# Differential attention with 64-row score contractions, one maximum and one ratio per head, and rotary and output gate moved ahead of the value products

## Chip, core and metric

The kernel runs on one core of a Trainium2 chip. All arithmetic is float32 in the matmuls. The metric is the device time of one execution in microseconds, lower is better; before the change the median of 3 runs is 1255.58 us (1250.82 to 1259.35).

## What is computed

A transformer block over 256 latent tokens and 256 context tokens of width 1024 (a token mixer of differential attention beside a gated recurrence, then 16 experts), followed by a second block (MLA and Fourier branches) that the change does not touch. Of the first mixer this matters here:

```python
def diff_attend(q, k, v, lam):       # 4 heads x 2 branches, head dim 64, value dim 128
    s = jnp.einsum("bhiqd,bhikd->bhiqk", q, k).astype(jnp.float32) * (DA_HEAD_DIM ** -0.5)
    p = jax.nn.softmax(s, axis=-1)
    a = p[:, :, 0] - lam * p[:, :, 1]
    return jnp.einsum("bhqk,bhkd->bhqd", a.astype(v.dtype), v)

q = apply_axial_rope(qk_heads(da_q), cos, sin)            # x*cos + rotated(x)*sin
k_all = concatenate([k_ctx, apply_axial_rope(qk_heads(da_k), cos, sin)])     # 512 keys
out_da = merge_heads(rmsnorm(o_da, da_subln) * (1.0 - lambda_init))
out_hg = merge_heads(rmsnorm(o_hg_lat, hg_norm)) * jax.nn.silu(hg_g)
y_lat = jnp.concatenate([out_da, out_hg], axis=-1) @ w_out
```

## The kernel before

Every engine has its own program, written out in order by hand; engines meet through semaphores. Eight PSUM banks of 128x512 float32 are handed out ahead of time: `claim(name, bank)` gives each use of a bank a turn, `pe_take` makes TensorE wait until the previous user of the bank has been copied (`freed`), `wait_filled` makes a reader wait for TensorE (`filled`), `wait_copied` waits for the copy. `pclaim` goes round banks 0 to 3.

Weights come as 2 MB tiles (128 x 8 x 512 float32) through SyncE's queue, which works through `stream` in order: tile i goes to ring slot i % 4 and is issued once the last reader of tile i-4 has run. Slots 4 and 5 are scratch (`scr`: gates, decays, `XFB`, `gb`) until the experts.

The mixer runs on TensorE in this order. After the gates, the recurrence's levels (`level(0)` to `level(7)`) are interleaved with the key and query projections and with `mod_step(k)`, which are products of the modulation matrix (`w_ada`, columns). Then come the value projection (`("v", b)`, weight tile 2), `cross` and `oh` (the recurrence's output), `mod_step(12)`, the rotation products `rot` (a constant 128x128 matrix against q and k), the output gate's projection `g` (weight tile 7), and the attention loop over `da`: 2 blocks of 128 queries x 4 heads, n = 0 to 7.

In the loop the step of head n is, on TensorE: four transposes of the weights a (`aT`), the scores of head n+2, `mod_gate(n-1)` (a row product of the modulation), the value product `o`, a piece of context work for the second block (`c2T`, `kvc`, `kvcT`, `kpcT`), and `mod_product(n)` (L778, a 2 MB tile of `w_ada`). ScalarE: copies `aT`, takes the two exponentials of head n+2 (L1440, with row sums), at a block's last head the four squares of `o`, context copies, and the copy of the modulation product (`take_mod`). VectorE: `da_difference(n+1)` (L1923 to L1929), `da_max(n+2)` (L1881, L1883), at n = 0 `output_gate(1)`, then `gate_rows(n-1)` (L1892, L1895), which frees the bank of `mod_gate`, and at a block's last head the norm of `o` (L1951), which waits for GpSimd's inverse root.

Each score of a branch contracts all 128 partitions: q lies with both branches one above the other, and `qh` and `smat` hold copies in which the other branch's 64 rows are zero. Two maxima and two reciprocals are taken for a head. The output gate is made from an exponential (L1426), a sum with 1, a reciprocal over 128x512 (L1584) and two multiplications per token block.

After the loop the mixed rows are transposed (`mixT`) and multiplied by `w_out` (`y`), the router runs, and from about 473 us 16 experts follow in a loop whose first iteration's weights are already in the ring and whose later ones stream in at about 410 GB/s.

## Time and profile before

| | |
|---|---|
| runs | 1255.58 us median, 1250.82 to 1259.35 |
| profiled execution, its own time | 1254.22 us |
| its span in the trace | 1252.4 us |
| TensorE busy over the span | 977.6 us (78%) |
| TensorE busy, 245 to 312 us (values, recurrence out, rotary, gate) | 61.11 of 67.00 us |
| TensorE busy, 312 to 394 us (attention loop) | 67.06 of 82.00 us |
| experts, 473 to 1180 us | DMA at 305 GB/s on average, 410 in most slices |
| VectorE, ScalarE, GpSimd busy over the span | 420.1, 208.9, 48.2 us |

"PEclk" in the windows is TensorE's granted clock as a share of full speed (1.0 is 2.4 GHz, 0.5 is 1.2 GHz). In a timeline a row is a merged run of like instructions: its start, its length, engine, line, operation, output<-input, shapes, count, and in brackets how long the engine had stood idle before it and who released it.

### The profile page before, as it was taken

To read this page: it belongs to the slowest core of one execution; us is meant where nothing else is said; L and a number is where in the kernel's file an instruction comes from. 1 tells how busy PE (TensorE), PEld (TensorE's weight loads), DVE (VectorE), ACT (ScalarE), POOL (GpSimd) and SP (SyncE) were. 2 spreads that over 40 slices of the span, in tenths; PEclk is the share of its full clock that TensorE was granted. 3 is DMA by queue.
4 is the path that set the end of the run, shared out by engine and by line. 5 is a ranking of instruction groups with operands and counts; after the bars stand their busy time and mean duration, and the time that the engine had idled before them with its cause. 6 is when DMAs were issued, how large, how long until landed. Compare 5 with 4: busy or idle time off the path is not lost.

```text
span 1252.4 us, 11145 instructions
## 1 busy us (share of the span) xinstructions
PE 977.6 (78%) x4368; PEld 483.6 (39%) x4368; DVE 420.1 (34%) x643; ACT 208.9 (17%) x426; POOL 48.2 (4%) x101
## 2 busy tenths in 40 slices
PE   4799989998887777566666666666665998998987
PEld 2666456654443442111111111111112764544843
DVE  1398244616741342111111111111224264411422
ACT  2123132312441211000000000000002033301010
POOL 0100000001010100000000000000001000000000
PEclk9899989998898878877777777777777999998999
DMA  9934253844639507999999999999997441023000
GB/s 355 330 134 167 102 201 133 304 153 150 231 133 391 211 1 283 410 409 410 410 409 410 410 410 410 409 410 410 409 410 289 155 152 68 1 85 117 1 1 33
DMA packets 102230, 310.44 MB, mean 248 GB/s; under 512 B 2705, under 2 KB 4932, under 8 KB 102068
## 3 DMA queue, kind: packets, MB, share of 16 engines
q1 hardware_dynamic: 99700, 301.04, 62.4%
q0 software_dynamic: 2496, 8.93, 2.0%
q8 instruction: 23, 0.38, 0.1%
q14 instruction: 11, 0.09, 0.0%
HBM read 308.91 MB, written 1.05 MB: 247 GB/s over the span
## 4 chain that ended last, share of the span: by engine, by line
PE 57%; DMA 29%; DVE 7%; SPq 2%; issue 2%; ACT 1%; POOL 1%; POOLq 0%; ACTq 0%; DVEq 0%
PE bank L760 39%; DMA ring<-w_up_dram 27%; PE bank L1091 7%; PE bank L778 3%; DMA ring<-w_ada_dram 2%; SPq L659 1%; PE bank L768 1%; PE bank L889 1%; PE bank L1107 1%; PE bank L788 1%; PE bank L974 1%; SPq L644 1%; PE bank L1196 1%; DVE state L2045 1%; PE bank L1219 1%
## 5 line engine op out<-in xcount | busy, mean ns | idle before, releaser
L1091 PE MATMUL bank<-ring,ilat 128*32 128x512 f32 x1024 | 140.4, 699 | 48.2 <-DMA ring<-w_up_dram 48.2
L1107 PE MATMUL bank<-ring,ilat 128*32 128x512 f32 x512 | 95.7, 915 | 11.7 <-ACT ilat L1507 11.7
L760 PE MATMUL bank<-ring,hT 128*128 128x512 f32 x224 | 101.9, 616 | 3.7 <-DVE gates L1850 2.0
L760 PE MATMUL bank<-ring,kT 128*128 128x512 f32 (+1 forms) x224 | 97.8, 598 | 5.2 <-DVE kT L1616 3.4
L2043 DVE TENSOR_SCALAR state<-state 64x512 f32<-64x512 f32 x16 | 6.7, 419 | 256.9 <-ACT state L1505 256.9
L1091 PEld LDWEIGHTS bank<-ring,ilat 128*32 128x32 f32 x1024 | 35.3, 124 | 149.0 <-issue 92.1
L1098 PE MATMUL bank<-const,state 128*128 128x128 f32 x64 | 17.9, 434 | 95.7 <-DVE state L2049 95.7
L760 PE MATMUL bank<-hT,ring 128*128 128x256 f32 (+1 forms) x320 | 86.4, 431 | 3.6 <-DVE hT L1654 3.6
L760 PEld LDWEIGHTS bank<-hT,ring 128*128 128x128 f32 x320 | 61.6, 194 | 28.3 <-issue 17.7
L1119 PE MATMUL bank<-state,ilat 128*128 128x512 f32 x128 | 58.7, 602 | 14.6 <-DVE state L2051 14.6
L760 PEld LDWEIGHTS bank<-ring,hT 128*128 128x128 f32 x224 | 43.9, 198 | 59.2 <-issue 57.3
L760 PEld LDWEIGHTS bank<-ring,kT 128*128 128x128 f32 x224 | 43.2, 194 | 58.3 <-issue 58.3
L778 PE MATMUL bank<-ring,act 128*32 128x512 f32 x384 | 51.5, 661 | 8.3 <-DMA ring<-w_ada_dram 5.6
L760 PE MATMUL bank<-kT,ring 128*128 128x256 f32 x256 | 55.7, 379 | 0.0
L1098 PEld LDWEIGHTS bank<-const,state 128*128 128x128 f32 x64 | 11.5, 217 | 112.0 <-DVE state L2049 112.0
L2051 DVE COPY state<-bank 128x512 f32<-128x512 f32 x16 | 11.1, 692 | 127.4 <-PE bank L1107 127.4
L2045 DVE RECIPROCAL state<-state 64x512 f32<-64x512 f32 x16 | 53.5, 3345 | 0.5
L1505 ACT ACTIVATE state<-bank 64x512 f32<-64x512 f32 x16 | 9.4, 590 | 262.3 <-PE bank L1091 262.3
L1107 PEld LDWEIGHTS bank<-ring,ilat 128*32 128x32 f32 x512 | 21.3, 158 | 78.0 <-issue 77.1
L760 PEld LDWEIGHTS bank<-kT,ring 128*128 128x128 f32 x256 | 48.6, 190 | 7.3 <-issue 0.8
L1119 PEld LDWEIGHTS bank<-state,ilat 128*128 128x128 f32 x128 | 23.0, 189 | 51.6 <-issue 51.6
L768 PE MATMUL bank<-const,pair 128*128 128x128 f32 x112 | 21.8, 361 | 26.6 <-DVE pair L1982 19.0
(319 smaller groups left out, 1096.3 us busy)
## 6 DMA issues: line engine op xcount, KB each, us to landing
ring<-w_down_dram SPq DMA_DIRECT2D x32, 2048.0 KB, 19.9
ring<-w_gate_dram SPq DMA_DIRECT2D x32, 2048.0 KB, 18.9
ring<-w_up_dram SPq DMA_DIRECT2D x32, 2048.0 KB, 23.0
ring<-w_ada_dram SPq DMA_DIRECT2D x24, 2048.0 KB, 11.6
ring<-w_in_dram SPq DMA_DIRECT2D x8, 2048.0 KB, 13.3
ring<-fno_w_in_dram SPq DMA_DIRECT2D x4, 2048.0 KB, 8.8
ring<-w_out_dram SPq DMA_DIRECT2D x2, 2048.0 KB, 15.5
ring<-mla_w_in_dram SPq DMA_DIRECT2D x2, 2048.0 KB, 21.8
```

What stands on the lines that cost most here:

```text
L644: sp.dma_start(slot_view(s, src.shape[1], src.shape[2]), src).then_inc(landed[s], 16)
L659: sp.dma_start(expert_view(s), expert_src(w, e, half)).then_inc(landed[s], 16)
L760: ins = pe.matmul(o, l, r, start=start and i == 0, stop=stop and i == len(terms) - 1)
L768: ins = pe.transpose(o[:, jj * P:(jj + 1) * P], src[:, j * P:(j + 1) * P], ident)
L778: ins = pe.matmul(o[32 * q:32 * q + 32, :], act_cols[i // 12][:, j, :], w[:, j, :], start=jj == 0, stop=jj == 1)
L788: ins = pe.matmul(o[:, 2 * jj:2 * jj + 2], x[:, jj * P:(jj + 1) * P], C("sum_columns"), start=True, stop=True)
L889: ins = pe.matmul(o[:, k * P:(k + 1) * P], keys[:, c:c + P], queries[:, c:c + P], start=True, stop=True)
L1091: ins = pe.matmul(bank[0][32 * t:32 * t + 32, :], xin_cur[:, j, :], w[2 * half + t // 2][:, j % JH, n0:n0 + TN], start=j == 0, stop=j == J ...
L1098: ins = pe.transpose(bank[1][:, k * P:(k + 1) * P], hidden_rows[:, k * P:(k + 1) * P], ident)
L1107: ins = pe.matmul(bank[2 + n][32 * q:32 * q + 32, :], hmT[:, q, 32 * c:32 * c + 32], w[4 + c][:, q, n * TN:(n + 1) * TN], start=c == 0, st ...
L1119: ins = pe.matmul(bank[4 + 2 * b + n][:, :], s_cur[:, b * P:(b + 1) * P], yb[n], start=False, stop=last)
L2045: dve.reciprocal(eg, eg).then_inc(hidden, 1)
```

## The change

Scores: each branch contracts its own 64 partitions of q and k directly (`q3[ps]`, `k3[ps]`, rows 0 to 63 and 64 to 127). The zero-padded copies and the memsets that made them are gone. The two score banks of a head are adjacent, so that one reduction over 2 x 512 gives both maxima and one exponent pair waits for it. The difference is scaled by one ratio: a' = p0 - lam*(s0/s1)*p1, not divided by s0; the RMS norm removes the factor s0, with EPS scaled by s0*s0 (`eps_sums`) in GpSimd's root.

Order: `rot` and `g` move ahead of the value projection, with weight tiles 7 and 2 swapped in the stream, and `mod_step(12)` and the first two heads' scores ahead of `cross` and `oh`. The rotary arithmetic moves ahead of `cross_ready` on VectorE. The gate becomes tanh: (1+tanh(x/2))*x*0.5*hg_norm, and is applied in the multiplication that normalises `oh` (`recurrent_out`), which moves into VectorE's loop iteration n = 0. `kvctx` leaves the four-slot ring for slot 4, so the `w_ada` tiles of heads 4 to 7 are loaded one head earlier. `o` moves to banks 5 and 6, context work to 6 and 5, the modulation products of the loop to bank 7. The squares and norm of `ctx_2`, and its load, move to the values stage and earlier.

```diff
-        for i, (name, _) in enumerate(stream):
-            place(name, i % EARLY_SLOTS)
+        for name, _ in stream:
+            if name[0] == "kvctx":
+                place(name, EARLY_SLOTS)
+            else:
+                place(name, turn % EARLY_SLOTS)
+                turn += 1
...
         for b in range(TB):
-            if b:
-                claim(("o", b), 7)
+            claim(("o", b), 5 + b)
             for h in range(HEADS):
                 n = b * HEADS + h
                 claim(("aT", b, h), 4)
-                if n == 0:
-                    claim(("o", 0), 6)
                 for name in context_work[n]:
-                    claim(name, 4 if name == ("kpcT",) else 5)
-                claim(("mod", GATE_MODS[n]), 7 - b)
-                claim(("gt", GATE_MODS[n]), 7 - b)
+                    claim(name, 4 if name == ("kpcT",) else 6 - b)
+                claim(("mod", GATE_MODS[n]), 7)
+                claim(("gt", GATE_MODS[n]), 7)
...
# TensorE
             def da_scores(b, h):
+                o = [pe_take(pe, ("s", b, h, i)) for i in range(2)]
                 for i in range(2):
-                    o = pe_take(pe, ("s", b, h, i))
-                    fills(pe.matmul(o[:, :], qz[i][:, h * T + b * P:h * T + (b + 1) * P], k3[:, h, :],
-                                    start=True, stop=True), ("s", b, h, i))
+                    ps = slice(64 * i, 64 * i + 64)
+                    fills(pe.matmul(o[i][:, :], q3[ps, h, b * P:(b + 1) * P], k3[ps, h, :],
+                                    start=True, stop=True), ("s", b, h, i))
...
# ScalarE
+            da_exp(0)
+            act.wait_ge(sem("rstd_c2"), 1)
+            act.wait_ge(sem("c2_normed"), TB)
+            for b in range(TB):
+                o = wait_filled(act, ("oh", b))
+                for h in range(HEADS):
+                    square(o[:, h * P:(h + 1) * P], 4 * b + h, P, (b, h) == (TB - 1, HEADS - 1))
...
-            da_exp(0)
             da_exp(1)
...
# VectorE
             def da_max(n):
                 for i in range(2):
-                    o = wait_filled(dve, ("s",) + da[n] + (i,))
-                    c = (2 * n + i) % 4
-                    step(dve.tensor_reduce(mx[:, 4 + c:5 + c], o[:, :], AX, ALU.max))
-                    st.settle()
-                    step(dve.tensor_scalar(mx[:, c:c + 1], mx[:, 4 + c:5 + c], -DH ** -0.5, None, ALU.mult), "da_max")
+                    wait_filled(dve, ("s",) + da[n] + (i,))
+                c = 2 * (n % 2)
+                step(dve.tensor_reduce(mx[:, 4 + c:6 + c],
+                                       score_banks[n % 2][:, :].rearrange("p (i t) -> p i t", i=2), AX, ALU.max))
...
-                step(dve.reciprocal(cf[:, c:c + 2], rs[:, c:c + 2]))
+                c = 2 * (n % 2)
+                step(dve.reciprocal(cf[:, c:c + 1], da_sums[:, 8 + n:9 + n]))
                 st.settle()
-                step(dve.tensor_tensor(cf[:, 4 + c:5 + c], cf[:, c + 1:c + 2], lamc, ALU.mult))
+                step(dve.scalar_tensor_tensor(cf[:, c + 1:c + 2], cf[:, c:c + 1], da_sums[:, n:n + 1], lamc,
+                                              ALU.mult, ALU.mult))
                 st.settle()
-                step(dve.tensor_scalar(pbuf[c + 1], pbuf[c + 1], cf[:, 4 + c:5 + c], None, ALU.mult))
-                st.settle()
-                step(dve.scalar_tensor_tensor(pbuf[c], pbuf[c], cf[:, c:c + 1], pbuf[c + 1], ALU.mult, ALU.add),
+                step(dve.scalar_tensor_tensor(pbuf[c], pbuf[c + 1], cf[:, c + 1:c + 2], pbuf[c], ALU.mult, ALU.add),
                      "a_ready")
...
                 if n == 0:
-                    output_gate(1)
+                    recurrent_out()
```

In TensorE's program of the kernel before, from the end of `mod_step(12)` to the first transposes (L788 is the modulation's column product, L962 `rot`, L760 here `g`, L974 the scores):

```order
L788 MATMUL bank<-const,modr 128x2 x4
L962 MATMUL bank<-qT,const 128x256 x4
L962 MATMUL bank<-kT,const 128x256 x4
L760 MATMUL bank<-ring,hT 128x512 x16
L974 MATMUL bank<-kT,qh 128x512
L974 MATMUL bank<-kT,smat 128x512
```

In TensorE's program of the changed kernel, from the last level (L907) to `cross` (L973); L942 is `rot`, the first L778 row `g` and the first two blocks of values, L959 the four scores of heads 0 and 1:

```order
L907 MATMUL bank<-qh,ring 128x128 x8
L942 MATMUL bank<-qT,const 128x256 x4
L942 MATMUL bank<-kT,const 128x256 x4
L778 MATMUL bank<-ring,hT 128x512 x32
L806 MATMUL bank<-const,vda 128x2 x4
L796 MATMUL bank<-ring,act 32x512 x8
L778 MATMUL bank<-ring,hT 128x512 x16
L806 MATMUL bank<-const,modr 128x2 x4
L959 MATMUL bank<-kT,qT 128x512 x4
L973 MATMUL bank<-ring 128x128 x8
```

What stood between the recurrence's output and the loop now stands before it: `cross` and `oh` follow the first scores directly, and the first transposes follow `oh`.

In ScalarE's program of the changed kernel, from the copies of `cross` (L1434) to the copy of the first modulation product of the loop (L1334); L1446 are the exponentials, L1299 the squares of `oh`, L1471 the copy of `aT`:

```order
L1434 ACTIVATE ring<-bank 128x512 x2
L1446 ACTIVATE gates,small<-bank,small 128x512 x2
L1299 ACTIVATE junk,small<-bank 128x128 x8
L1446 ACTIVATE gates,small<-bank,small 128x512 x2
L1471 ACTIVATE gates<-bank 128x512
L1446 ACTIVATE gates,small<-bank,small 128x512 x2
L1334 ACTIVATE gates<-bank 128x512
```

The squares of `oh` now stand between the exponentials of head 0 and those of head 1; before, they stood ahead of both and four copies of the gate's projection lay between.

In VectorE's program of the changed kernel, from the maximum of head 2 (L1895) to the difference of head 2 (L1935 to L1940); L1881 is the eightfold normalisation and gating of `oh`:

```order
L1895 TENSOR_REDUCE small<-bank 128x2
L1898 TENSOR_SCALAR small<-small 128x2
L1881 SCALAR_TENSOR_TENSOR pair<-bank,small,ring 128x128 x8
L1887 MEMSET small 128x1
L1935 RECIPROCAL small<-small 128x1
L1937 SCALAR_TENSOR_TENSOR small<-small 128x1
L1940 SCALAR_TENSOR_TENSOR gates<-gates,small 128x512
```

Where the gate's sum, reciprocal and multiplications stood (L1582 to L1872 of before), the reading of `oh` out of banks 6 and 7 stands now.

## Rows read from the trace of the kernel before

**Rows 1.** Windows: length; PE, PEld, DVE, ACT, POOL busy; PEclk, DMA share, GB/s.

```profile
245.00:312.00 67.00, 61.11 (x230) 33.96 (x230) 26.95 (x38) 12.57 (x32) 5.60 (x7) 0.95 0.49 173
312.00:394.00 82.00, 67.06 (x341) 34.94 (x340) 42.74 (x99) 33.88 (x90) 8.00 (x14) 0.88 0.64 223
473.00:1180.00 707.00, 513.07 (x2437) 214.75 (x2436) 177.86 (x238) 77.16 (x164) 20.72 (x47) 0.84 0.77 305
```

**Rows 2.** Timeline of TensorE before the loop: start, length, line, shapes, idle before.

```profile
245.49 13.90 PE L760 MATMUL bank<-ring,hT 128*128 128x512 f32 x32
292.49 1.10 PE L962 MATMUL bank<-kT,const 128*128 128x256 f32 x4 [3.15 <-DVE modc L1637]
295.60 16.82 PE L760 MATMUL bank<-ring,hT 128*128 128x512 f32 x32 [2.01 <-DVE gates L1850]
```

**Rows 3.** Timeline of TensorE in the loop.

```profile
318.41 1.11 PE L1004 MATMUL bank<-const,gates 128*128 128x128 f32 x4 [2.56 <-DVE gates L1929]
332.45 3.39 PE L778 MATMUL bank<-ring,act 128*32 128x512 f32 x16 [2.77 <-DVE hT L1892]
335.78 0.66 PE L1004 MATMUL bank<-const,gates 128*128 128x128 f32 x4
342.12 0.66 PE L1004 MATMUL bank<-const,gates 128*128 128x128 f32 x4
342.62 1.02 PE L974 MATMUL bank<-kT,qh 128*128 128x512 f32 x2
346.62 1.92 PE L778 MATMUL bank<-ring,act 128*32 128x512 f32 x16
348.47 0.66 PE L1004 MATMUL bank<-const,gates 128*128 128x128 f32 x4
354.64 1.13 PE L760 MATMUL bank<-vda,gates 128*128 128x128 f32 x8 [2.93 <-DVE hT L1892]
```

**Rows 4.** The same, from the last head to the output product.

```profile
376.15 0.66 PE L1004 MATMUL bank<-const,gates 128*128 128x128 f32 x4
382.49 2.94 PE L778 MATMUL bank<-ring,act 128*32 128x512 f32 x16 [2.27 <-DMA ring<-w_ada_dram]
389.94 3.65 PE L768 MATMUL bank<-const,pair 128*128 128x128 f32 x16 [1.60 <-DVE qT L1912]
394.58 1.95 PE L760 MATMUL bank<-ring,kT 128*128 128x512 f32 x4 [0.99 <-ACT kT L1474]
```

**Rows 5.** Windows with and without a lowered clock.

```profile
295.00:302.00 7.00, 6.40 (x9) 2.75 (x10) 6.90 (x8) 2.30 (x4) 1.83 (x2) 0.55 0.03 8
336.00:354.00 18.00, 15.71 (x86) 7.84 (x84) 11.89 (x30) 11.53 (x33) 1.27 (x2) 1.00 0.90 312
```

**Rows 6.** Timeline of ScalarE and VectorE, end of the levels.

```profile
246.90 1.22 DVE L1815 TENSOR_TENSOR ring<-gates 128x1024 f32<-128x1024 f32 x1
249.64 0.58 ACT L1317 ACTIVATE vda<-bank 128x512 f32<-128x512 f32 x1
```

**Rows 7.** Timeline of ScalarE, VectorE and GpSimd: pieces of a head's chain.

```profile
344.54 0.69 DVE L1881 TENSOR_REDUCE small<-bank 128x1 f32<-128x512 f32 x1
340.38 0.16 DVE L1923 RECIPROCAL small<-small 128x2 f32<-128x2 f32 x1
341.30 0.75 DVE L1929 SCALAR_TENSOR_TENSOR gates<-gates,small 128x512 f32<-128x512 f32 x1
344.65 0.69 ACT L1440 ACTIVATE gates<-bank,small 128x512 f32<-128x512 f32 x1 [1.24 <-DVE small L1883]
290.12 2.16 DVE L1837 SCALAR_TENSOR_TENSOR pair<-bank,small,hgn 128x128 f32<-128x128 f32 x8 [29.75 <-POOL small L695]
348.33 1.04 POOL L695 TENSOR_TENSOR small<-small 128x4 f32<-128x4 f32 x1
```

**Rows 8.** DMA issues of GpSimd: KB each, us to landing.

```profile
state<-norm_post_ffn_dram POOLq DMA_DIRECT2D x1, 512.0 KB, 6.8
```

**Rows 9.** Chain that ended last, at the loop's end.

```profile
374.39 8.05 DMA ring<-w_ada_dram
```

More of the change, by code:

```diff
@@ L174, in block_program @@
         ident = C("ident")
-        bank = [ctx.enter_context(nc.psum_tensor(f"bank{b}", [P, TN], F32)) for b in range(8)]
+        score_banks = [ctx.enter_context(nc.psum_tensor(f"bank{2 * i}", [P, 2 * TN], F32)) for i in range(2)]
+        bank = [x[:, i * TN:(i + 1) * TN] for x in score_banks for i in range(2)]
+        bank += [ctx.enter_context(nc.psum_tensor(f"bank{b}", [P, TN], F32)) for b in range(4, 8)]
         filled = [sem(f"filled{b}") for b in range(8)]
@@ L337, in block_program @@
         ecol = small[:, 96:128]
+        da_sums = small[:, 96:112]
+        eps_sums = small[:, 112:116]
         lbt = small[:, 128:152]
@@ L418, in block_program @@
         claim_levels(7)
+        for s in range(2):
+            for n in range(2):
+                pclaim(("rot", s, n))
+        for b in range(TB):
+            pclaim(("g", b))
         pclaim(("v", 0))
@@ L429, in block_program @@
             lb_turn[0] += 1
-        claim_mod(12)
-        for s in range(2):
-            for n in range(2):
-                pclaim(("rot", s, n))
-        for b in range(TB):
-            pclaim(("g", b))
         context_work = [(), (("c2T", 0, 0),), (("c2T", 0, 1),), (("c2T", 1, 0),), (("c2T", 1, 1),),
@@ L712, in _ @@
             root_inverse(TB, TB, "rstd_in")
+            for b in range(TB):
+                wait_filled(pool, ("dsum", 1, b))
+            pool.dma_start(c2, a["ctx_2"][0].rearrange("(b p) d -> p b d", p=P)).then_inc(sem("ctx2_in"), 16)
+            root_inverse(0, TB, "rstd_c2")
+            wait_filled(pool, ("v", 2 * TB - 1))
+            for i, row in enumerate((a["b_ada"][0, 2 * D:3 * D], a["b_ada"][0, 5 * D:6 * D],
+                                     a["b_ada_2"][0, 2 * D:3 * D], a["b_ada_2"][1, 2 * D:3 * D])):
+                pool.dma_start(G[i], row.partition_broadcast(P)).then_inc(sem("post_in"), 16)
             wait_filled(pool, ("oh", TB - 1))
@@ L914, in _ @@
             level(7)
+            for s, x in enumerate((q3, k3)):
+                for n in range(2):
+                    if s == 0:
+                        wait_copied(pe, ("q", n))
+                    else:
+                        wait_copied(pe, ("k", 2 * n))
+                        wait_copied(pe, ("k", 2 * n + 1))
+                    o = pe_take(pe, ("rot", s, n))
+                    for i in range(2):
+                        ins = pe.matmul(o[:, i * T:(i + 1) * T], C("rotate"), x[:, 2 * n + i, 0:T],
+                                        start=True, stop=True)
+                    fills(ins, ("rot", s, n))
+            w = wait_tile(pe, ("in", 7))
+            for b in range(TB):
+                tokens_out(("g", b), w, hT3, b)
             w = wait_tile(pe, ("in", 2))
@@ L1403, in _ @@
             take_mod(COLUMN_MODS[10])
+            for b in range(TB):
+                o = wait_filled(act, ("g", b))
+                st.did(act.activation(gb[:, b * TN:(b + 1) * TN], o[:, :], ACT.Tanh, scale=0.5), sem("gb_tanh"))
             for b in range(2 * TB):
@@ L1408, in _ @@
                     take_mod(COLUMN_MODS[11])
+                    act.wait_ge(sem("ctx2_in"), 16)
+                    for i in range(TB):
+                        square(c2[:, i, :], i, D, i == TB - 1)
             for d in range(2):
@@ L1464, in _ @@
                     if b == 0:
-                        act.wait_ge(sem("rstd_c2"), 1)
+                        act.wait_ge(sem("rstd_oh"), 1)
+                        for i in range(TB):
+                            wait_copied(act, ("oh", i))
                     for i in range(HEADS):
@@ L1830, in _ @@
                                        .broadcast_to([P, HEADS, P]), ALU.mult), "state1_ready" if d else None)
+            for b in range(TB):
+                g_ = gb[:, b * TN:(b + 1) * TN]
+                dve.wait_ge(sem("gb_tanh"), b + 1)
+                frees(st, dve.scalar_tensor_tensor(g_, g_, 1.0, bank[turns[("g", b)][0]][:, :], ALU.add, ALU.mult),
+                      ("g", b))
+                st.settle()
+                g4 = g_.rearrange("p (h n) -> p h n", h=HEADS)
+                step(dve.scalar_tensor_tensor(g4, g4, 0.5, hgn[:, :].rearrange("p (h n) -> p h n", h=1)
+                                              .broadcast_to([P, HEADS, P]), ALU.mult, ALU.mult))
@@ L1912, in take_context @@
                     frees(st, dve.tensor_copy(kp_ctx, o[:, 0:T]), ("kpcT",))
-            dve.wait_ge(sem("rstd_c2"), 1)
-            for b in range(TB):
-                step(dve.tensor_scalar(c2[:, b, :], c2[:, b, :], rr[:, b:b + 1], None, ALU.mult), "c2_normed")
             def da_difference(n):
```

172 lines of the change are left out of this document (73 added, 99 removed).

## Prediction

> **What bounds the kernel now.** I read the windows by stage first. In the two stages that the change touches TensorE is busy 61.11 of 67 us and 67.06 of 82 us, with the granted clock at 0.95 and 0.88 of full speed, while VectorE has 26.95 and 42.74 us of work [rows 1]. So TensorE's program sets the pace, and what can be won is its idle time, the time at a lowered clock, and work taken from it. The experts behind are another matter: 707 us in which DMA moves 305 GB/s [rows 1] and whose weights are asked for as the previous ones are used up. Their start follows the end of the mixer one for one, so a microsecond won before 394 us is one won at the end.
>
> Next the timeline of TensorE. Ahead of the loop it idles 3.15 us because the last `rot` product needs a bank that VectorE has not emptied, and 2.01 us in front of `g` for the same reason; `g` then takes 16.82 us where the first half of the value product, the same 32 instructions, takes 13.90 [rows 2]. The window shows why: the clock is at 0.55 of full speed there, between the levels 1.2 and 2.4 GHz, and at 1.00 where no such gap stands [rows 5]. At the loop's start it idles 2.56 us for the first difference, in head 1 2.77 us (`output_gate(1)` with its long reciprocal holds up `gate_rows`), in head 4 2.93 us [rows 3]. After two of these gaps the modulation product takes 3.39 instead of 1.92 us, or the start of a head is stretched likewise [rows 3]. Heads 2 and 3 have no wait: 335.78 to 342.12 to 348.47, so 6.35 us is what one head's work costs [rows 3]. At the end the last modulation product waits 2.27 us for its tile, asked for only at 374.39 and 8.05 us under way [rows 4, 9], then runs slow (2.94), and `mixT` needs 3.65 us for 16 transposes after a wait of 1.60 [rows 4].
>
> **The change, step by step.** I carry TensorE's position from 245.49 us and compare it at four marks.
>
> *Up to the first transposes (before: 318.41).* The work on TensorE is the same as before except the scores. Before, idle time is 3.15 + 2.01 + 2.56 [rows 2, 3], and the slow `g` cost 16.82 - 13.90 = 2.9. Gone is 10.6 us. New waits: the fourth `rot` product needs the bank of modulation product 10, which ScalarE copies at 249.64 + 0.58 = 250.2, behind the exponentials that wait for VectorE at 246.90 + 1.22 [rows 6]. Three `rot` products of 0.86 us from 245.5 end at 248.1, so 2.2 us idle. A gap of 2.2 us lies near the 2.0 and 2.8 that went with a lowered clock [rows 2, 3]; I count 1.5 us for that. The scores of two heads: one of 512 columns lasts 0.86 us (its two passes are 1.02 with the tail [rows 3]). The two branches now use separate halves of the array's rows. The nearest row is the modulation product: 16 instructions of 512 columns on separate groups of 32 columns last 1.92 us in all [rows 3], 0.12 each, where one on the full array costs 0.43; four run side by side. So I take it that the halves overlap: 0.86 instead of 1.72 us per head, here -1.7. Both ends for each head: 0 and -0.86. The rotary arithmetic on VectorE (six operations, 7.4 us) and the gate's (four of 0.75) lie under 41 us of `g` and value products; without that cover they would cost 10 us. Sum: -10.6 + 2.2 + 1.5 - 1.7 = -8.6, and half a microsecond for the slow start of head 0 (its transposes took 1.11 instead of 0.66 [rows 3]); the maximum, exponential and difference of head 0 now lie under `oh`. Mark: 309.3, **-9.1**.
>
> *Heads 0 and 1 (before: 318.41 to 335.78, 17.4).* The bulk of VectorE's gate arithmetic is gone, with the waits of 2.77 and the slow clock after it. In its place: `oh` is complete at 309.3 and everything of the loop hangs on ScalarE. Squares of the second `oh` 1.6, exponentials of head 1 1.6 (two of 0.69 with accumulator reads [rows 7]), copy of `aT` 0.6: 313.1, so the value product of head 0 waits 2.4 us. VectorE has the exponentials at 312.5, the difference 1.15 (0.16 + 0.16 + 0.75 and gaps [rows 7]), the maximum of head 2 over 2x512 elements: 1.4 (the row of 512 takes 0.69, of which some 0.15 is fixed; between 1.2 and 1.4 [rows 7]), then the eight multiplications of `oh`, 2.16 by the row of the same form [rows 7], to 317.4. These free bank 7, for which modulation product 0 waits: before, `oh` was out of bank 7 at 292. So TensorE idles a further 2.5 us there, and 1.5 us goes for the clock. GpSimd's root (1.04 for four columns [rows 7], up to 2 for eight) stands behind three DMA issues, ends at about 313.5 and is not the last. Modulation product 0 ends at 320.9, head 1 takes 5.5 us: 326.5. That is 17.2 us, **-0.2**: one stall was traded for another.
>
> *Heads 2 to 6 (before: 335.78 to 376.15, 40.4).* Heads 2 and 3 lose 0.8 each by the overlapped scores; head 5 too. Head 4 keeps its stall. The chain is squares of `o`, root (1.04 [rows 7] and the sum ahead of it, 1.4), four multiplications and then difference, maximum and `gate_rows(3)`. It starts 0.6 us later on ScalarE against TensorE than before because both exponentials now wait for both scores, but what waits for it is no longer `o` but the modulation product, 1.3 us further on, and VectorE's pieces are 0.7 us shorter. I get an idle of 1.35 + 1.71 instead of 2.93, without a single long gap: -2.6, the slow clock included. Head 6: 0. Mark: 362.0, together **-4.9**.
>
> *End of loop to output product (before: 376.15 to 394.58, 18.4).* The tile of the last product is now asked for after head 3 instead of head 4, so 25 us ahead: -2.27 and the slow product -1.1. The row product behind it no longer lies at the lower clock (-1.2). The wait for the last copies (1.60) and for ScalarE (0.87, 0.99) stay. `mixT` at full speed would take 1.9 instead of 3.65; since these small gaps stay I count half. **-6.3**.
>
> Sum: -9.1 - 0.2 - 4.9 - 6.3 = -20.5. From the execution's own 1254.2 us: 1233.7. The median of the runs lies 1.4 above the profiled one: **1235 us**.
>
> Priced at nothing, with their cover: the tanh (ScalarE's program as built holds no table load more than before, and ScalarE is busy 12.57 of 67 us in this stage [rows 1]), the load of `ctx_2`, now at about 128 us, and its squares and norm, under the value product; at the loop's start they would cost 5 us.
>
> **The rivals.**
>
> *The two score products do not overlap.* For it: no row here has a contraction of 64, only column groups. The Trainium skill, "TensorEngine Tiling (Array Packing)", Key Properties, states that tiles execute in parallel, but also that changing the tiling mode drains the engine. By the first rule the sum stands at -20.5; by the second each head, which now changes mode twice more, would pay for it. The trace bears the drain out little: head 2's 6.35 us hold two changes to 128x32 and back and add up from the single rows without a remainder above 0.1 us [rows 3]. Without overlap all scores together cost 0.86 x 8 = 6.9 more; some of it falls into waits that exist anyway (2 us), leaving 5: 1240 us.
>
> *Fewer stalls than counted.* The gaps of 2.2 and 2.5 us leave the clock alone and `mixT` runs fast: 1.5 + 1.5 + 0.9 us more: 1231 us.
>
> *The new order's waits cost more at head 0 and in each block.* ScalarE carries in each head a copy, two exponentials that start only after a reduction over both banks, a context copy of 1.5 and the modulation copy: 4.9 of 5.5 us. If these slip by 1.2 us in six heads and with them the clock: +9 us, 1244 to 1248, within 1%.
>
> *Slower than before.* `gate_rows(0)` waits for six broadcast loads, two of which GpSimd issues only after `oh`, now 309.5 us, with the router's and the 768 KB context tile behind them. The slower of them was seen to land after 6.8 us [rows 8], so at 317, and is wanted at 324. Every microsecond past 324 holds bank 7, and with it TensorE, one for one. It decides when the landing takes 20 us more than wanted (344, no gain left), and makes 1268 us when it lands at 357. A whole 2 MB tile took 8.05 us [rows 9]; three such ahead of the rows would put the landing at 334, which costs 10 us and does not yet reach the old time.
>
> **How the numbers follow.** My sum 0.50; no overlap 0.18; fewer stalls 0.14; more waits 0.14; slower 0.04. Within 1% of 1255.6 is 1243 to 1268, about what a measurement of this kernel can tell from no change. Faster: the first three, 0.82 less 0.02 for their tails; same: the fourth and these tails, 0.16; slower 0.04. The range takes the fast rival's 1231 less 3 for the spread of runs, and up to the middle of the fourth: 1228 to 1245.
>
> **What the profile will show.** Right: the first transposes at 308 to 311 us, the output product's start at 372 to 377, score pairs of 0.9 to 1.1 us for both branches, the last modulation product without a DMA wait. At head 0 a wait of 2 us or more for ScalarE's copy and another on the VectorE row that normalises `oh`. Wrong: pairs of 1.7 us; a wait in `cross` for the rotary arithmetic; a wait of `gate_rows(0)` for DMA; an expert loop that does not move with the mixer's end.

## The result, and the profile after

The changed kernel takes 1235.58 us (median; 1234.59 to 1237.53), against 1254.62 us (1250.82 to 1259.35) for the kernel before beside it: a ratio of 0.985, 95% interval 0.981 to 0.989, so 19 us or 1.5% faster. Forecast were 1235 us and 1228 to 1245. The profiled execution has a span of 1232.8 us (before 1252.4) and its own time of 1234.59. How much of the agreement is merit is the subject of what follows: in the part of the program that the change touches the sum had promised 20.5 us and 16.8 came.

The windows of the changed kernel (length; busy time of PE, PEld, DVE, ACT, POOL; PEclk, DMA share, GB/s), to be held against [rows 1]:

```profile
245.00:312.00 67.00, 64.06 (x250) 35.83 (x249) 23.73 (x34) 13.81 (x36) 4.38 (x9) 0.97 0.51 185
312.00:379.00 67.00, 54.47 (x326) 29.86 (x327) 30.79 (x75) 30.20 (x85) 7.21 (x12) 0.92 0.91 329
473.00:1180.00 707.00, 509.43 (x2438) 224.64 (x2430) 184.15 (x242) 79.27 (x167) 19.95 (x45) 0.86 0.76 299
```

From 312 us to the output product are now 67 us instead of 82 (the second window ends where that stage ends), with 12.5 us of TensorE idle instead of 15, at 0.92 of full clock instead of 0.88; VectorE's work in this window fell from 42.74 to 30.79 us. These windows don't hold the same work: at 312 us the kernel before had only reached the first scores, the changed one was past the first transposes. So the 15 us are not the gain of the loop; the table below compares like with like. The experts' window has hardly changed.

TensorE's timeline of the changed kernel (start, length, line, shapes, count, idle before and its releaser), which answers to [rows 2] to [rows 4]:

```profile
250.81 2.05 PE L942 MATMUL bank<-kT,const 128*128 128x256 f32 x4 [2.12 <-ACT vda L1334]
...
298.33 1.99 PE L959 MATMUL bank<-kT,qT 64*128 64x512 f32 x8
300.25 2.05 PE L973 MATMUL bank<-ring 128*128 128x128 f32 x16
...
310.25 0.60 PE L1021 MATMUL bank<-const,gates 128*128 128x128 f32 x4
310.78 1.13 PE L959 MATMUL bank<-kT,qT 64*128 64x512 f32 x4
314.10 1.16 PE L778 MATMUL bank<-vda,gates 128*128 128x128 f32 x8 [2.19 <-ACT gates L1471]
318.42 3.64 PE L796 MATMUL bank<-ring,act 128*32 128x512 f32 x16 [3.16 <-DVE pair L1881]
...
328.07 0.66 PE L1021 MATMUL bank<-const,gates 128*128 128x128 f32 x4
328.66 1.13 PE L959 MATMUL bank<-kT,qT 64*128 64x512 f32 x4
329.72 1.13 PE L814 MATMUL bank<-modr,const 128*128 128x512 f32 x2
330.68 1.05 PE L778 MATMUL bank<-vda,gates 128*128 128x128 f32 x8
...
342.41 1.10 PE L814 MATMUL bank<-modr,const 128*128 128x512 f32 x2 [0.85 <-ACT modr L1334]
346.25 1.92 PE L796 MATMUL bank<-ring,act 128*32 128x512 f32 x16 [1.42 <-DVE hT L1907]
...
364.17 0.66 PE L1021 MATMUL bank<-const,gates 128*128 128x128 f32 x4
368.17 1.92 PE L796 MATMUL bank<-ring,act 128*32 128x512 f32 x16
373.68 3.58 PE L786 MATMUL bank<-const,pair 128*128 128x128 f32 x16 [1.60 <-DVE qT L1927]
378.25 3.24 PE L778 MATMUL bank<-ring,kT 128*128 128x512 f32 x7 [0.99 <-ACT kT L1488]
```

In place of the 3.15 and 2.01 us ahead of the loop stands one gap of 2.12, in place of 2.56 and 2.77 in heads 0 and 1 stand 2.19 and 3.16, in place of 2.93 in head 4 stand 0.85 and 1.42, and the wait of 2.27 for a tile at the end is gone.

The start of a kernel differs from one trace to the next (the last level, from which I count below, starts between 243.6 and 249.0 us in twelve traces), and so do the experts. Only the changed kernel was traced twice, with starts 0.26 us apart, so whether the start goes by the execution or by the kernel is not shown. Places in the mixer are compared by their distance from the start of the last level, 243.60 us before and 244.05 after; these distances are called marks below.

| mark: us from the last level to | before | after | stage before | stage after | stage forecast |
|---|---|---|---|---|---|
| transposes of head 0 | 74.81 | 66.20 | | -8.6 | -9.1 |
| transposes of head 2 | 92.18 | 84.02 | 17.37 | 17.82 (+0.45) | -0.2 |
| transposes of head 7 | 132.55 | 120.12 | 40.37 | 36.10 (-4.3) | -4.9 |
| output product `y` | 150.98 | 134.20 | 18.43 | 14.08 (-4.35) | -6.3 |

The mixer gained 16.8 us. From `y` to the first expert it is 79.09 and 79.04 us, so the experts' start followed one for one. The other 3 us of this trace come from the experts, 2.3 of them from TensorE's clock in the last one (its down product took 6.19 and 5.60 us, and the up product as follows); the same products of that expert before (L1091) and after (L1108), from the two timelines:

```profile
931.78 5.34 PE L1091 MATMUL bank<-ring,ilat 128*32 128x512 f32 x32 [3.37 <-DMA ring<-w_up_dram]
```

```profile
914.81 3.64 PE L1108 MATMUL bank<-ring,ilat 128*32 128x512 f32 x32 [2.70 <-DMA ring<-w_up_dram]
```

The shapes and the count are the same and the change doesn't touch the line; after a wait for the tile of 3.37 us it ran slow in one trace, after one of 2.70 at full clock in the other (in the earlier experts of the changed kernel's trace the up products run slow and fast by turns). From the first expert to the last one's final product it is 478.12 us before and 475.24 after; in the ten other traces 475.1 to 477.8, in no order with the mixer's length.

### The profile page after: what moved, and what is told of

The parts are those of the page before. It is cut to its first block, busy times and chain, and to the rows that moved or that the text cites. A ratio compares the mean times of both kernels' runs of the same rounds, so it can differ in the third digit from the quotient of the medians.

```text
span 1232.8 us, 11161 instructions
## 1 busy us (share of the span) xinstructions
PE 954.5 (77%) x4368; PEld 479.7 (39%) x4368; DVE 404.6 (33%) x615; ACT 206.4 (17%) x424; POOL 47.0 (4%) x101
## 3 DMA queue, kind: packets, MB, share of 16 engines
HBM read 308.91 MB, written 1.05 MB: 251 GB/s over the span
## 4 chain that ended last, share of the span: by engine, by line
PE 57%; DMA 29%; DVE 6%; SPq 3%; issue 2%; ACT 2%; POOL 1%; POOLq 0%; ACTq 0%; DVEq 0%
PE bank L778 39%; DMA ring<-w_up_dram 27%; PE bank L1108 7%; PE bank L796 3%; SPq L671 2%; DMA ring<-w_ada_dram 2%; PE bank L907 1%; PE bank L786 1%; PE bank L1124 1%; PE bank L806 1%; SPq L653 1%; PE bank L1213 1%; DVE state L2060 1%; PE bank L1236 1%; PE bank L1136 1%
## 5 line engine op out<-in xcount | busy, mean ns | idle before, releaser
L1108 PE MATMUL bank<-ring,ilat 128*32 128x512 f32 x1024 | 133.2, 668 | 57.7 <-DMA ring<-w_up_dram 57.7
L778 PE MATMUL bank<-ring,kT 128*128 128x512 f32 (+1 forms) x224 | 97.6, 597 | 5.4 <-DVE kT L1630 3.4
L778 PE MATMUL bank<-ring,hT 128*128 128x512 f32 x224 | 99.6, 605 | 1.7 <-DVE hT L1630 1.7
L1124 PE MATMUL bank<-ring,ilat 128*32 128x512 f32 x512 | 90.5, 872 | 11.8 <-ACT ilat L1521 11.8
L1108 PEld LDWEIGHTS bank<-ring,ilat 128*32 128x32 f32 x1024 | 35.5, 121 | 153.0 <-issue 153.0
L778 PE MATMUL bank<-hT,ring 128*128 128x256 f32 (+1 forms) x320 | 86.6, 432 | 3.6 <-DVE hT L1668 3.6
L778 PEld LDWEIGHTS bank<-hT,ring 128*128 128x128 f32 x320 | 62.0, 196 | 28.3 <-issue 17.7
L778 PEld LDWEIGHTS bank<-ring,kT 128*128 128x128 f32 x224 | 43.1, 194 | 58.0 <-issue 58.0
L778 PEld LDWEIGHTS bank<-ring,hT 128*128 128x128 f32 x224 | 43.5, 195 | 56.1 <-issue 54.0
L778 PE MATMUL bank<-kT,ring 128*128 128x256 f32 x256 | 55.7, 379 | 0.0
L1115 PEld LDWEIGHTS bank<-const,state 128*128 128x128 f32 x64 | 11.4, 217 | 110.1 <-DVE state L2064 110.1
L778 PEld LDWEIGHTS bank<-kT,ring 128*128 128x128 f32 x256 | 48.7, 190 | 7.2 <-issue 0.8
L1124 PEld LDWEIGHTS bank<-ring,ilat 128*32 128x32 f32 x512 | 20.5, 154 | 73.6 <-issue 72.7
## 6 DMA issues: line engine op xcount, KB each, us to landing
ring<-w_down_dram SPq DMA_DIRECT2D x32, 2048.0 KB, 20.5
```

Source lines behind the costliest of these rows:

```text
L778: ins = pe.matmul(o, l, r, start=start and i == 0, stop=stop and i == len(terms) - 1)
L1108: ins = pe.matmul(bank[0][32 * t:32 * t + 32, :], xin_cur[:, j, :], w[2 * half + t // 2][:, j % JH, n0:n0 + TN], start=j == 0, stop=j == J ...
L1115: ins = pe.transpose(bank[1][:, k * P:(k + 1) * P], hidden_rows[:, k * P:(k + 1) * P], ident)
L1124: ins = pe.matmul(bank[2 + n][32 * q:32 * q + 32, :], hmT[:, q, 32 * c:32 * c + 32], w[4 + c][:, q, n * TN:(n + 1) * TN], start=c == 0, st ...
```

## The experiments

My theory: each stall is set by one instruction of another engine that stands behind work nobody waits for, and the change traded six of them (3.15 + 2.01 + 2.56 + 2.77 + 2.93 + 2.27 = 15.7 us) for five (2.12 + 2.19 + 3.16 + 0.85 + 1.42 = 9.7 us), beside the overlapped scores. First rival: the gain is nearly all work taken from TensorE, and the waits float, that is, a wait that is removed comes back at the next place, so that moving one instruction moves nothing. Second rival: what counts is the clock, and waits matter only where they lower it. Kernels with "from before" are the kernel before with one part of the change; the others are the changed kernel with one edit.

### Scores over 128 rows again

```diff
-                    fills(pe.matmul(o[i][:, :], q3[ps, h, b * P:(b + 1) * P], k3[ps, h, :],
+                    fills(pe.matmul(o[i][:, :], q3[:, h, b * P:(b + 1) * P], k3[:, h, :],
```

> The changed kernel with both score products of a head contracting all 128 rows (both branches get the same scores, so the output differs); instruction shapes are those of the kernel before, all else as changed. Theory: the two 64-row halves run side by side, so a head's pair now lasts 0.96 to 1.06 us and would last 1.72 again: +1.5 us for heads 0 and 1 ahead of the recurrence's output, nothing for head 2 (TensorE waits there anyway), +0.66 for most of heads 3 to 7. The output product starts 4 to 5 us later (382 to 383 us) and the time is 1239 to 1241 us. Rival, the loop's pace is set by ScalarE and VectorE: under 2 us later, 1236 to 1238 us.

1241.72 us (1239.87 to 1242.12), a ratio to before of 0.989 (0.987 to 0.992): 4 to 6 us behind the changed kernel's two medians (1235.58 above, 1237.57 below). This kernel serves for its timing alone: it leaves out the separation of the two branches. TensorE in head 2, and `mixT` at the end:

```profile
332.50 0.66 PE L1021 MATMUL bank<-const,gates 128*128 128x128 f32 x4
333.00 1.88 PE L959 MATMUL bank<-kT,qT 128*128 128x512 f32 x4
334.72 1.02 PE L814 MATMUL bank<-modr,const 128*128 128x512 f32 x2
335.58 1.05 PE L778 MATMUL bank<-vda,gates 128*128 128x128 f32 x8
...
379.82 1.94 PE L786 MATMUL bank<-const,pair 128*128 128x128 f32 x16 [1.60 <-DVE qT L1927]
```

Start to start, both branches take 1.72 us here and 1.06 in the changed kernel (328.66 to 329.72); two heads in one go take 1.92 there (298.33 to 300.25). One head more costs 0.86, what one branch over 128 rows costs: the halves run fully side by side, and 0.20 us is paid once for each group. There is more around it: the scores start 0.59 us after the transposes instead of 0.50, and the row product behind them takes 0.96 instead of 0.86 (329.72 to 330.68, here 334.72 to 335.58). So going to 64 rows and back costs 0.20 + 0.09 + 0.10 = 0.39 us, and a head saves 0.46 us instead of 0.86. The Trainium skill, "TensorEngine Tiling (Array Packing)", Key Properties, says both that tiles run in parallel and that a change of mode drains the engine; this trace agrees with both: complete overlap, and 0.39 us for each excursion. That these 0.39 us are the drain is a reading; the trace shows only the time.

By the marks `y` is at 134.55, only 0.35 later than in the changed kernel. Heads 2 and 3 cost 1.24 us more (0.92 by the rows above, and 0.15 each ahead of the modulation product, which the kernel before did not have; I can't say why), heads 4 to 6 0.47, heads 0 and 1 0.36; against that the fourth `rot` product ran at full speed behind the same gap of 2.12 us (1.10 instead of 2.05), and `mixT` took 1.94 instead of 3.58 behind the same 1.60. With the clock set aside the 64 rows are worth about 3.4 us in this order, an estimate from these differences. The 4 to 5 us expected at `y` did not come in this trace; its 0.35 lies in the rival's range, but the rows show longer work on TensorE hidden by a higher clock, and not a pace set by other engines. This execution took 6.9 us longer than the changed kernel's profiled one, nearly all of it elsewhere: 4.3 us in the start-up, 0.5 in the experts and 2.2 in the second block, none of which the edit touches. So the trace does not explain the distance between the medians.

### The context tile back in the ring

```diff
-                if name[0] == "kvctx":
-                    wait_filled(sp, ("oh", TB - 1))
-                elif turn_of[name]:
+                if turn_of[name]:
```

(and the same condition taken out where the slots are placed.)

> The changed kernel with kvctx back in the ring of four slots. Theory: the tile of the last modulation product is again asked for only when kvctx's last reader has run (head 6), lands 8 us later, about 370.4, where it is wanted at 368.2: a DMA wait of 2.2 us in front of the last modulation product, a slow product behind it (2.9 us), output product 3 to 6 us later. Rival, the tile's wait is hidden by the copies at the loop's end: under 1 us.

One execution: 1242.93 us. All marks up to head 7 agree with the changed kernel within 0.03 us; then comes the wait:

```profile
372.17 3.50 PE L792 MATMUL bank<-ring,act 128*32 128x512 f32 x16 [2.17 <-DMA ring<-w_ada_dram]
```

`y` is at 137.84, 3.64 later: 2.17 of wait, 1.6 of slow product. The rest of the distance in time is start-up (1.7), experts (0.9) and the second block (2.2), which this edit doesn't reach.

### The copy of modulation product 10 first

```diff
+            take_mod(COLUMN_MODS[10])
             act.wait_ge(sem("end_distance"), 1)
...
-            take_mod(COLUMN_MODS[10])
```

> The changed kernel with ScalarE's copy of modulation product 10 ahead of its wait for the end distances. Theory: the wait of 2.12 us of the fourth rotation product goes, and with it the lowered clock behind it (1.7 us): first transposes 3.8 us earlier, about 306.4, time about 1232. Rival, the clock falls for another reason than the gap: 2.1 us earlier, with the rotation and gate products as slow as now.

One execution: 1235.46 us. The `rot` products now run without a gap:

```profile
249.69 1.03 PE L942 MATMUL bank<-kT,const 128*128 128x256 f32 x4
```

Head 0 is reached at 62.19 instead of 66.20: 4.0 us, 2.1 of wait and the rest the clock behind it; 3.9 of them still stand at `y`. The time doesn't show it, since this execution started 1.2 us later and its experts and second block took 1.2 and 2.2 us longer. By the marks it contradicts the first rival; the time alone, at 1235.46 us for about 1232 expected, would not.

### The gap at head 0 filled with unread products

```diff
                     context_product(*name)
+                if n == 0:
+                    for i in range(2):
+                        wait_copied(pe, ("s",) + da[1] + (i,))
+                    for i in range(3):
+                        pe.matmul(bank[2][:, :], q3[:, 0, 0:P], k3[:, 0, :], start=True, stop=True)
                 mod_product(GATE_MODS[n])
```

> The changed kernel with three matmuls of 512 columns that nothing reads put into the wait in front of modulation product 0. Theory: the idle gap of 3.16 us is what brings the clock down to 1.2 GHz; filled, the product takes 1.92 instead of 3.64 us and the next transposes 0.6 instead of 0.86: head 1 begins 1.9 to 2.0 us earlier. Rival, the clock comes down anyway: the product still takes over 3 us, nothing gained.

One execution: 1235.71 us.

```profile
318.38 2.74 PE L1039 MATMUL bank<-kT,qT 128*128 128x512 f32 x6
321.71 1.93 PE L796 MATMUL bank<-ring,act 128*32 128x512 f32 x16 [0.58 <-DVE pair L1886]
323.56 0.66 PE L1021 MATMUL bank<-const,gates 128*128 128x128 f32 x4
```

VectorE releases the bank no sooner (the modulation product starts 4.32 us after the value product, as without the edit), but it takes 1.93 instead of 3.64 us: heads 0 and 1 together 15.91 instead of 17.82, as expected. This separates the price of a wait from the price of the clock: the stall cost 3.16 us and 1.9 in clock.

### Head 0: exponentials first, root before the loads, norm of `oh` before the maximum

```diff
# ScalarE
             da_exp(0)
+            da_exp(1)
...
# GpSimd: ahead of the last three DMA issues
+            root_inverse(0, TB * HEADS, "rstd_oh")
             wait_filled(pool, ("oh", TB - 1))
...
# VectorE
-                if n + 2 < len(da):
-                    da_max(n + 2)
                 if n == 0:
                     recurrent_out()
+                if n + 2 < len(da):
+                    da_max(n + 2)
```

> The changed kernel with three pieces of order changed around head 0: ScalarE takes the exponentials of head 1 ahead of the squares of the recurrence's output, VectorE normalises that output ahead of the maximum of head 2, GpSimd takes its root ahead of three DMA issues. Theory: TensorE's two waits (2.19 and 3.16 us) are queue order on ScalarE, VectorE and GpSimd; bank 7 comes free about 2 us earlier and modulation product 0 starts at 316.4 instead of 318.4, still slow. Rival, squares and root are one chain that order doesn't shorten: under 1 us.

One execution: 1237.11 us.

```profile
315.37 1.16 PE L778 MATMUL bank<-vda,gates 128*128 128x128 f32 x8 [0.85 <-ACT gates L1471]
319.20 3.64 PE L796 MATMUL bank<-ring,act 128*32 128x512 f32 x16 [2.67 <-DVE pair L1881]
322.77 1.12 PE L1021 MATMUL bank<-const,gates 128*128 128x128 f32 x4
323.82 1.72 PE L959 MATMUL bank<-kT,qT 64*128 64x512 f32 x4
```

The value product waits 0.85 instead of 2.19, and with bank 7 free sooner the modulation product starts 6.34 us after head 0 instead of 8.17: the 2 us expected there, nearly. But the gap in front of the modulation product is still 2.67, since TensorE also arrives earlier, and the low clock now lasts into head 1 (1.12 and 1.72 for what took 0.86 and 1.13). Of 1.8 us won in the waits 0.97 is left at head 2. The three edits were made together, so what each gave is not shown.

### The last copies before the last gate row

```diff
-            gate_rows(len(da) - 1)
-
             take_context("kvcT")
             take_context("kpcT")
+
+            gate_rows(len(da) - 1)
```

> The changed kernel with VectorE's copies of kvcT and kpcT ahead of the last gate row. Theory: the transposes of the mixed rows wait 1.60 us for bank 4, which these copies free; they start 1.6 us earlier, and the output product 1.6 to 3.3 us earlier, depending on whether the clock stays up. Rival, another bank or ScalarE's copy decides: nothing.

One execution: 1234.94 us.

```profile
375.58 1.94 PE L786 MATMUL bank<-const,pair 128*128 128x128 f32 x16 [0.25 <-DVE qT L1927]
378.67 1.52 PE L778 MATMUL bank<-ring,kT 128*128 128x512 f32 x3 [1.15 <-ACT kT L1488]
```

Head 7 to `y` takes 11.26 instead of 14.08 us: 1.35 of the wait and 1.64 of `mixT` at full clock, less 0.16 of a longer wait for ScalarE. By the marks `y` comes 4.0 us earlier, but 1.66 of that lie ahead of head 0, where this trace has the same gap and a fast `rot` product (1.10 us); the edit has no part in it. This end was the same in both kernels; neither the change nor my forecast had touched VectorE's order there.

### From before: the context tile outside the ring, alone

```diff
+            if name[0] == "kvctx":
+                place(name, EARLY_SLOTS)
+            else:
+                place(name, turn % EARLY_SLOTS)
+                turn += 1
```

> The kernel before with only the ring changed: kvctx in slot 4, tiles of heads 4 to 7 one place earlier. Theory: the DMA wait of 2.27 us in front of the last modulation product goes, with its slow product (1.1) and part of what is slow behind it (1.2 and 1.8): 3.4 to 6 us, 1249 to 1251. Rival, hidden by the last copies: under 1 us.

1250.57 us (1247.75 to 1252.04), ratio 0.996 (0.995 to 0.998), 3.6 us.

```profile
384.88 1.92 PE L790 MATMUL bank<-ring,act 128*32 128x512 f32 x16
390.39 1.94 PE L780 MATMUL bank<-const,pair 128*128 128x128 f32 x16 [1.60 <-DVE qT L1924]
```

No wait for the tile, and `mixT` at 1.94 instead of 3.65 [rows 4]: head 7 to `y` 12.61 instead of 18.43, by the marks 6.1 us. 1.7 of them are `mixT` at full clock, which the changed kernel did not get. The medians show 3.6; the profiled execution started 5.0 us later than that of before and its second block took 1.7 longer.

### From before: the 64-row scores alone

```diff
-                    fills(pe.matmul(o[:, :], qz[i][:, h * T + b * P:h * T + (b + 1) * P], k3[:, h, :],
+                    ps = slice(64 * i, 64 * i + 64)
+                    fills(pe.matmul(o[:, :], q3[ps, h, b * P:(b + 1) * P], k3[ps, h, :],
```

(q is rotated in place; the memsets go.)

> The kernel before with only the 64-row scores: q rotated in place, no zero-padded copies, no memsets. Theory: pairs of 1.0 instead of 1.72 us in 8 heads, some of it absorbed by the two stalls (4 to 5 us), and VectorE reaches the first rotation product 1.8 us earlier, which takes the 2.01 us wait and some of the slow clock from the gate product (2 to 4 us): 6 to 9 us, 1246 to 1249. Rival, only the scores count: 4 to 5 us.

1245.52 us (1244.75 to 1248.7), ratio 0.994 (0.993 to 0.996), 8.6 us; by the marks 5.0 at head 0 and 6.9 at `y`.

```profile
293.91 13.96 PE L760 MATMUL bank<-ring,hT 128*128 128x512 f32 x32
313.84 1.11 PE L1005 MATMUL bank<-const,gates 128*128 128x128 f32 x4 [3.68 <-DVE gates L1925]
327.76 1.92 PE L778 MATMUL bank<-ring,act 128*32 128x512 f32 x16 [2.88 <-DVE hT L1888]
348.10 2.05 PE L760 MATMUL bank<-vda,gates 128*128 128x128 f32 x8 [3.52 <-DVE hT L1888]
```

The wait of 2.01 in front of `g` [rows 2] is gone with the two memsets (0.91 us each) that stood on VectorE ahead of the rotary arithmetic, and with it the slow `g` (13.96 instead of 16.82). The shorter scores are partly eaten by the stalls: 3.68, 2.88 and 3.52 us where [rows 3] has 2.56, 2.77 and 2.93.

### The changed kernel again

> The changed kernel once more, unaltered. Theory: the stretch from the last level to the output product repeats within 2 us (134.2), its spread being whether the gaps of the same length bring the clock down; start-up (243.6 to 249.0 us seen), expert loop (475 to 478) and end (300.2 or 302.4) vary on their own; 1235 to 1237 us. Rival, all stretches repeat within 0.5 us and the differences seen belonged to the kernels.

1237.57 us (1234.29 to 1238.78), ratio 0.987 (0.986 to 0.989). In the profiled execution the marks are 66.18, 83.99, 120.09 and 134.16, within 0.05 us of the first, down to the slow `rot` product:

```profile
250.55 2.04 PE L942 MATMUL bank<-kT,const 128*128 128x256 f32 x4 [2.12 <-ACT vda L1334]
```

But marks repeat this well only where the clock does. Five more of these kernels have the changed kernel's order on TensorE up to head 0, with the same gap of 2.11 to 2.12 us. In those with the context tile in the ring and with the new order at head 0, the first transposes stand at 66.21 and 66.20; in those with unread products and with the last copies first, where the `rot` product took 1.10 us, at 64.54; the one with 128-row scores, also with a fast `rot`, is at 65.96 with its longer scores. So half a microsecond between marks means something where the clock was the same, and one such product at the other clock moves all marks behind it by 1.7 us. Totals move by 3 us and more. The 17.1 us between the medians here agree with the 16.8 at `y`.

### Everything that helped, and one more

`mod10`, `head0` and `tail` together, the root once per token block so that the first is ready while `oh` still runs, and `gate_rows(3)` ahead of the maximum of head 6:

```diff
+                if n == HEADS:
+                    gate_rows(n - 1)
+                if n + 2 < len(da):
+                    da_max(n + 2)
```

> The changed kernel with all orders mended: copy of modulation product 10 early; exponentials of head 1 ahead of the squares; the root of the recurrence's output taken per token block and ahead of the DMA issues, its normalisation ahead of the maximum of head 2; gate row 3 ahead of the maximum of head 6; last copies ahead of the last gate row. Theory, from the marks against the last level: first transposes -4.0, head 2 a further -2.5 to -4 (bank 7 free 4 us after the recurrence's output instead of 8), head 4 -0.7 to -1.4, output product -1.6 to -3.3: it starts 9 to 12 us earlier than in the changed kernel, time 1224 to 1227. Rival, the clock takes back what the waits give: 5 to 7 us, 1229 to 1231.

1230.46 us (1227.81 to 1231.56), ratio to before 0.981 (0.979 to 0.982), 7.1 us under the changed kernel of the same comparison; 8.0 at `y`. That misses the 9 to 12 us and the 1224 to 1227 expected, and the time is the rival's. The rival's reason, that the clock takes back what the waits give, holds at one place, that of the last row here.

```profile
311.49 1.16 PE L779 MATMUL bank<-vda,gates 128*128 128x128 f32 x8 [0.85 <-ACT gates L1472]
313.63 1.92 PE L797 MATMUL bank<-ring,act 128*32 128x512 f32 x16 [0.98 <-DVE pair L1882]
321.48 1.92 PE L797 MATMUL bank<-ring,act 128*32 128x512 f32 x16 [1.85 <-DVE hT L1908]
345.71 2.04 PE L815 MATMUL bank<-gates,const 128*128 128x512 f32 x2 [1.92 <-ACT gates L1335]
```

Head 0 comes 4.0 us earlier, heads 0 and 1 take 14.35 instead of 17.82, head 7 to `y` 11.27. The gate row in front of the maximum backfired: the 1.42 in head 4 is gone, but the exponentials of head 6 now start later, ScalarE's modulation copy with them, and TensorE waits 1.92 in head 5 and runs slow. Heads 4 to 6 take 26.64 instead of 24.33, of which about 1.6 is the lower clock behind that wait (2.04 and 1.80 us for 1.13 and 1.05). Without this edit `y` should stand another 2 us earlier; that wasn't run.

## Why the forecast was right, and where its steps failed

*The frame.* TensorE's order as the path, and the end following the mixer one for one, held: 79.09 and 79.04 us from `y` to the first expert, and 17 to 19 us in time against 16.8 at `y`. The first transposes at 310.25 lie in the 308 to 311 named, but `y` at 378.25 lies outside the 372 to 377. The sum was 3.7 us too large in the mixer; the experts gave 3 back, most of it the clock in the last of them, which no step had foreseen. That 1235 was met so closely is luck; the direction and the size of the mixer's gain (16.8 of 20.5 us) are not. The median of the second series, 1237.6, is what 16.8 us would give.

*Up to head 0 (-9.1; -8.6).* The gap of 2.2 for ScalarE's copy came as 2.12 and cost 1.7 in clock, for 1.5 counted (0.95 in `rot`, 0.76 in the 64 products behind: 28.39 us, and 27.63 in the kernel with unread products, where `rot` ran fast). The two heads' scores took 1.92, not 1.72. The tanh, priced at nothing, brought no table load: ScalarE has five in either trace, all before 240 us.

*Heads 0 and 1 (-0.2; +0.45).* One stall was traded for another, as said. ScalarE's copy came to the moment (a wait of 2.19 for 2.4 forecast). The bank 7 stall was 3.16, not 2.5, for which ScalarE, VectorE and GpSimd show:

```profile
313.45 0.59 ACT L1471 ACTIVATE gates<-bank 128x512 f32<-128x512 f32 x1
...
313.66 0.16 DVE L1935 RECIPROCAL small<-small 128x1 f32<-128x1 f32 x1 [8.08 <-ACT gates L1446]
314.78 1.22 DVE L1895 TENSOR_REDUCE small<-bank 128x2 f32<-128x1024 f32 x1
316.11 2.16 DVE L1881 SCALAR_TENSOR_TENSOR pair<-bank,small,ring 128x128 f32<-128x128 f32 x8
...
313.07 1.67 POOL L709 TENSOR_TENSOR small<-small 128x8 f32<-128x8 f32 x1
```

The reduction over two banks took 1.22 (forecast 1.2 to 1.4), the root ended at 314.7 and was not the last, as said; VectorE ended at 318.3 instead of 317.4 because ScalarE handed over its exponentials 1 us later than I had counted (313.5 for 312.5).

*Heads 2 to 6 (-4.9; -4.3).* This step failed in size. A head without a wait went from 6.35 to 5.89 us, 0.46 less and not 0.8. I had the overlap right and had let the change of mode go at under 0.1 us, because two changes to 128x32 in head 2 had left no remainder [rows 3]; those could not show it, as lengths taken from the same trace already contain whatever the changes cost. It costs 0.39 us each time. The rival without overlap is refuted; the price of the change of mode, which the Trainium skill states as a drain ("TensorEngine Tiling (Array Packing)", Key Properties), is what was missing. Head 4 waited 0.85 + 1.42 us for 1.35 + 1.71 forecast, which gave a quarter of a microsecond back.

*Loop's end to `y` (-6.3; -4.35).* The wait for the tile (2.27) and the slow product (1.0) went, as the kernels with and without the ring change show from both sides (6.1 us in before, 3.6 in after). The reason I gave was wrong in one point: the tile was not late by one head's turn. It lay in the slot of the context tile, whose last reader is the context product of head 6, and that is why it was asked for only at 374.39 [rows 9]. `mixT` was counted half fast and was wholly slow (3.58), 0.9 us; the row product behind the tile gave 0.9, not 1.2. And the items of this step add up to 5.5 us, not to the 6.3 that I put down: 0.8 us of the miss is plain addition.

*The rivals.* Fewer stalls: no, the two gaps and `mixT` were slow. More waits: no; in the loop no head but 0 and 4 waits over 0.5 us. Slower through late rows for `gate_rows(0)`: no such wait stands in the trace.

*Theory and rivals.* Moving one instruction moved TensorE at the product of ScalarE's copy (4.0 us), at head 0 (1.0) and at the loop's end (2.8), so waits do not float. The second rival is half right: behind the bank 7 gap the clock was 1.9 of some 5 us, and at the end 1.6 of 2.8. By TensorE's rows the 16.8 us are of three kinds: 6.0 us less idle in the waits listed with the theory, about 6 less at the lower clock (some 11.4 us before, in `g`, heads 0, 1 and 4 and at the loop's end, against 5.2 after, in `rot`, at the end of head 0 and in `mixT`), and 4.3 from shorter scores (1.5 for heads 0 and 1, 0.46 for each of the six others). So work taken from TensorE is a quarter of the gain. From before, the 64 rows give 6.9 and the ring 6.1 us at `y`, 13.0 of 16.8; the remaining 3.8 (5.5 without the ring kernel's fast `mixT`) is what order, gate and banks brought on top, if the parts add up. It was not run by itself. It is so little because it brought new waits of 2.12, 2.19 and 3.16.

What stays open is why a gap of one length lowers the clock in one trace and not in another (below).

## What to carry over

In a kernel whose programs are written out by hand, list for each stall which instruction releases it and what stands ahead of that on its engine without being waited for; such moves, each of a line or two, gave 7 us here after the change had given 17 to 19. Before moving one, look at the next waiter of what it pushes back: the one edit made without that cost 2.3 us. And judge parts by marks within the touched stage, since here they repeat within 0.05 us while totals move by 3; but see first that the same products ran at the same clock, since one that did not moved the marks by 1.7.

## What the runs showed of the hardware

- Two products over 64 rows each, in different halves of the array, run side by side (0.86 us for both, as for one over 128 rows), and going to such products and back costs 0.39 us, so pairs should be grouped: two heads in one go took 1.92 us, one 1.06.
- The same `rot` gap of 2.11 to 2.12 us was followed by a product at the lower clock in the changed kernel and its repetition (2.05, 2.04 us) and by one at full clock with 128-row scores (1.10) and here:

```profile
255.77 1.10 PE L942 MATMUL bank<-kT,const 128*128 128x256 f32 x4 [2.11 <-ACT vda L1339]
```

  That is from the kernel with unread products, whose program up to there is that of the changed kernel. In all, four traces have this product slow (last level at 243.8 to 246.7 us) and three fast (248.4 to 249.0): the fast ones are those that started latest. Whether the start is the reason no run tells. The 1.60 us ahead of `mixT` likewise: 3.37 to 3.65 us in seven traces, 1.94 with 128-row scores, with the new order at head 0 and in before with the ring change, and there the start does not sort them. The changed kernel repeated its own pattern; what decides it isn't settled.
- With three unread products in a gap of 3.16 us the clock stayed up and 1.9 us were won.
- Start-up moved between 243.6 and 249.0 us, the experts between 475.1 and 478.1, the second block between 300.1 and 302.5, whatever the edit in the mixer.
